# Gating one head later and dividing the next panel later, inside a projection woven with gated linear attention

## The reference

```
h = half_ffn(h, ..., w_up[0], w_down[0]);  hc likewise        # SwiGLU
n = modulate(rms_norm(h));  p = split(n @ w_in)               # q k v | gq gk gv gz | low | gate
attn = block_attention(rope(rms(q)), [rope(rms(k_lat)), rms(k_ctx)], v)
gla  = gla_chunked(forward) + flip(gla_chunked(backward))     # 4 heads, dk 64, dv 128
gla  = rms_norm(gla, g_gla) * silu(gz)
h = h + gate * ((sig(g0)*(attn @ wb0) + sig(g1)*(gla @ wb1)) @ w_out)
h = half_ffn(h, ..., w_up[1], w_down[1]);  return rms_norm(h)
```

## Time and profile before

| | us |
|---|---|
| median of 3 runs | 2684.03 (2683.47 to 2684.93) |
| profiled execution, its own time | 2686.08 |
| its span, first to last instruction | 2684.3 |
| TensorE busy | 2617.3 (98%) |
| VectorE busy | 1557.8 (58%) |
| ScalarE busy | 755.7 (28%) |
| GpSimd busy | 619.1 (23%) |
| mean granted TensorE clock | 0.992 |

### The profile page before, as it was taken

The page is one execution under the profiler, slowest core; times in us unless marked ns, Lnnn a source line. Parts: engine busy times, 40 slices in busy tenths (PEclk is TensorE's granted clock), DMA queues, the critical chain, the costliest instruction groups (busy, mean ns, idle before and its releaser), DMA issues.

```text
span 2684.3 us, 36625 instructions
## 1 busy us (share of the span) xinstructions
PE 2617.3 (98%) x14328; PEld 2170.7 (81%) x14328; DVE 1557.8 (58%) x2445; ACT 755.7 (28%) x1293; POOL 619.1 (23%) x600
## 2 busy tenths in 40 slices
PE   7999999999999999999999989999999999999998
PEld 5888888888888877877777778888778888888887
DVE  5545554444434446347674578886548666666665
ACT  3100000000000024233346568772023223222224
POOL 1064456554540000003440027560000000000001
PEclk8999999999999999999999999999999999999999
DMA  6322112222221103112224210004501111111122
GB/s 228 117 67 67 63 52 83 91 75 95 71 79 40 40 19 115 55 59 60 71 77 127 92 48 1 1 17 157 157 16 47 47 51 60 56 52 47 47 63 87
DMA packets 198293, 187.73 MB, mean 70 GB/s; under 512 B 7645, under 2 KB 149770, under 8 KB 198026
## 3 DMA queue, kind: packets, MB, share of 16 engines
q1 hardware_dynamic: 190160, 171.83, 20.2%
q10 hardware_dynamic: 7994, 13.97, 1.4%
HBM read 161.39 MB, written 24.38 MB: 69 GB/s over the span
## 4 chain that ended last, share of the span: by engine, by line
PE 89%; DVE 5%; ACT 3%; issue 1%; DMA 1%; ACTq 0%; POOL 0%; SPq 0%; DVEq 0%; POOLq 0%
PE psum L222 21%; PE psum L223 21%; PE psum L224 21%; PE psum L1089 5%; PE psum L1090 5%; PE psum L1087 5%; PE psum L2408 2%; PE psum L2428 1%; PE psum L2427 1%; PE psum L2018 1%; DVE ptl L2535 1%; ACT pth L2484 1%; PE psum L2382 1%; PE psum L2383 1%; PE psum L430 1%
## 5 line engine op out<-in xcount | busy, mean ns | idle before, releaser
L222 PE MATMUL psum<-nh,wh 128*128 128x512 f32 (+2 forms) x1688 | 629.7, 373 | 6.1 <-DVE nl L569 5.0
L223 PE MATMUL psum<-nl,wh 128*128 128x512 f32 (+2 forms) x1688 | 614.7, 364 | 0.0
L224 PE MATMUL psum<-nh,wl 128*128 128x512 f32 (+2 forms) x1688 | 614.1, 364 | 0.0
L222 PEld LDWEIGHTS psum<-nh,wh 128*128 128x128 f32 (+1 forms) x1688 | 317.9, 188 | 71.2 <-issue 10.8
L223 PEld LDWEIGHTS psum<-nl,wh 128*128 128x128 f32 (+1 forms) x1688 | 318.0, 188 | 52.8 <-issue 4.1
L224 PEld LDWEIGHTS psum<-nh,wl 128*128 128x128 f32 (+1 forms) x1688 | 317.5, 188 | 52.7
L222 PE MATMUL psum<-hidh,wh 128*128 128x512 f32 (+1 forms) x880 | 329.7, 375 | 2.6 <-DVE h L895 2.0
L223 PE MATMUL psum<-hidl,wh 128*128 128x512 f32 (+1 forms) x880 | 326.4, 371 | 0.0
L224 PE MATMUL psum<-hidh,wl 128*128 128x512 f32 (+1 forms) x880 | 325.4, 370 | 0.0
L862 ACT ACTIVATE silu_a<-psum 128x512 f32<-128x512 f32 (+1 forms) x66 | 34.7, 527 | 836.1 <-PE psum L224 836.1
L197 DVE CAST wh<-raw 128x1024 fp32r<-128x1024 f32 (+1 forms) x111 | 83.0, 748 | 322.0 <-PE psum L224 321.8
(11 more groups left out here) (345 smaller groups left out, 4757.5 us busy)
## 6 DMA issues: line engine op xcount, KB each, us to landing
raw<-in_w_ffn_up_dram SPq DMA_DIRECT2D x88, 512.0 KB, 3.9
mod_part<-in_w_mod_dram SPq DMA_DIRECT2D x96, 256.0 KB, 4.2
raw<-in_w_ffn_down_dram SPq DMA_DIRECT2D x44, 512.0 KB, 3.4
raw<-in_w_in_dram SPq DMA_DIRECT2D x34, 512.0 KB, 3.8
mod_raw<-in_w_mod_dram SPq DMA_DIRECT2D x12, 1024.0 KB, 10.6
gates_saved<-staged ACTq DMA_DIRECT2D x40, 256.0 KB, 2.0
merge_gate<-gates_saved SPq DMA_DIRECT2D x8, 1024.0 KB, 5.4
x_rows<-in_x_dram SPq DMA_DIRECT2D x8, 512.0 KB, 8.4
```

The costliest lines, as they stand in the source:

```text
L222: pe.matmul(o, hi_w, hi_x, start=first, stop=False)
L223: pe.matmul(o, hi_w, lo_x, start=False, stop=False)
L224: return pe.matmul(o, lo_w, hi_x, start=False, stop=last)
```

## The change

Two things move in VectorE's stream; no instruction is added or taken away. The second head of each group (par 1) is gated two half-units later, at `OUT_SLOTS` + 7 = 95, 104, 113, 122; the first stays where both were. And the split of the next panel, which stood ahead of all pieces of a panel's first half-unit, now stands behind them, ahead of those of the second half-unit.

```diff
@@ win_dve
         for u in range(PAIR_UNITS, N_UNITS):
             i, c = win_units[u]
-            if c == 0 and i + 1 < len(win):
-                split_panel(dve, pn(panel0 + i + 1), KT * win[i + 1][1])
             for h in (2 * u, 2 * u + 1):
                 decay_dve(dve, h)
                 state_dve(dve, h)
                 intra_dve(dve, h)
                 qk_dve(dve, h)
                 first_dve(dve, h)
+                if h == 2 * u and c == 0 and i + 1 < len(win):
+                    split_panel(dve, pn(panel0 + i + 1), KT * win[i + 1][1])
@@ intra_dve
-        if h - 5 in OUT_SLOTS:
-            g = OUT_SLOTS.index(h - 5)
-            dve.wait_ge(z_loaded, 16 + 32 * (g + 1))
-            for par in range(2):
+        for par, later in ((0, 5), (1, 7)):
+            if h - later in OUT_SLOTS:
+                g = OUT_SLOTS.index(h - later)
+                dve.wait_ge(z_loaded, 16 + 32 * (g + 1))
                 dve.wait_ge(o_rs, 2 * g + par + 1)
                 dve.wait_ge(g_oc, 2 * g + par + 1)
                 nc.vector.scalar_tensor_tensor(gla_f[:, par, :], gla_f[:, par, :], cols_b[:, B_GGLA:B_GGLA + 1],
```

## The result

| | before | after |
|---|---|---|
| median of 7 runs, us | 2684.03 (2682.11 to 2685.68) | 2691.93 (2690.31 to 2695.16) |
| span of the profiled execution | 2684.3 | 2689.0 |
| its own time | 2686.08 | 2690.77 |
| mean granted clock | 0.992 | 0.994 |

The ratio of the times is 1.0027, with a 95% interval of 1.0018 to 1.0037: slower, by 7.9 us of medians.

A forecast was written before the change was run, and what follows sets the result against it. TensorE, with 89% of the chain of waits, was taken as the bound. The terms -4.1 + 1.3 + 0.5 + 1.4 + 5.7 gave +4.8 us, set against the median 2684.03: 2688.8, range 2681.0 to 2693.5.

The forecast's parts named there:

- h=82 to 87: Panels at h=82 and 86: splits hidden before now delay h=83 and h=87; +1.3 us, from +0.2 to +1.8.
- h=94 to 97: Group 0: the 3.42 us stall and slow clock go, smaller stalls come at h=95 and 96; -4.1 us.
- h=102 to 105: Group 1: the 1.41 us stall at h=103 grows by up to 0.7; +0.5 us, from -0.4 to +1.2.
- h=110 to 115: Group 2: the split loses ScalarE's cover at h=110, making h=111 late; +1.4 us, from +0.4 to +2.0.
- h=122, 123: Group 3: late store delays the rope table, stalling h=123's permutation 4.3 us plus slow clock; +5.7, from +2.2 to +7.2.
- The rule of shared interfaces: Moved splits: GpSimd and VectorE contend for SBUF interfaces, so splits put into GpSimd's work are dear; about 0.7 us a place.
- The rule that an idle array falls to half clock: TensorE at h=123: an idle array drops to half clock, so the new stall pays twice; 2.4 us added.
- my bound for a change that can be told: Whole kernel: 0.2%, 5.4 us, is about what a measurement tells from no change.
- (a): The forecast: h=94's stall traded for one at h=123, plus small ones at splits; 2686 to 2691.5, chance 0.55.
- (b): Slower by more: splits cost 2.6 or more each, rope table late, clock falls; +9.2, 2693, chance 0.30.
- (c): Rope table in time by 1444.0, no stall at h=123; -0.9, 2683.1, or 2681.4 with all h=94 gained; chance 0.15.
- (d): The change does nothing; rejected because VectorE's order changes at nine panels; no separate chance given.

The follow-up runs named there:

- fewer_splits: The whole change, but the last group's heads both gated at h=120 and the splits of h=82, 86, 110 left ahead of their pieces: 2682.84 us, ratio 0.9991.
- before_again: The kernel before, unchanged, run once more for a second profile: 2683.36 us (one run).
- placed: Kernel before with second heads of groups 0 and 1 late and only h=94's split moved, behind the pieces of h=97: 2681.41 us, ratio 0.9988.
- placed2: As placed, with the split of h=86 also moved, behind the pieces of h=88: 2680.78 us, ratio 0.9984 against the kernel before.
- h94_only: Kernel before with only group 0's second head gated at h=95 and h=94's split behind its pieces: 2682.07 us, ratio 0.9991.
- all_again: The whole changed kernel run once more, against the kernel before: 2691.31 us, ratio 1.0026.
- rope_ahead: The whole change with the last group's heads in swapped order and the rope loads issued ahead of the last store: 2686.25 us, ratio 1.0004 against before.
- g3_only: Kernel before with only the last group's second head gated at h=122 instead of 120, splits as before: 2690.36 us, ratio 1.0020.
- gates_only: Kernel before with all four second heads gated two half-units later, every split left ahead: 2692.85 us, ratio 1.0026.
- splits_only: Kernel before with every split moved behind its panel's first pieces, both heads gated at one place as before: 2688.42 us, ratio 1.0011.

## Why the prediction was right, and where a size was off

**What bounds the kernel.** Right: TensorE still holds most of the chain of waits (the page of the changed kernel, to be read against the earlier trace rows):

```profile
PE 87%; DVE 6%; ACT 3%; issue 2%; DMA 2%; ACTq 0%; POOL 0%; SPq 0%; DVEq 0%; POOLq 0%
```

**The terms**, read as the shift of TensorE's items between the two profiled executions, place by place:

| place | predicted | after against before |
|---|---|---|
| h=82 to 87 | +1.3 | +1.8 |
| h=94 to 97 | -4.1 | -3.4 |
| h=102 to 105 | +0.5 | +0.3 |
| h=110 to 115 | +1.4 | +1.4 |
| h=122, 123 | +5.7 | +5.7 |
| sum | +4.8 | +5.8 |

The third row is read up to the output of h=106; at h=105 itself it was +0.6.

From h=81 (1253.60 and 1252.37) to h=128's permutation (1467.21 and 1471.91) it is 213.61 before and 219.54 after, +5.9. At h=81, ahead of all these places, the changed kernel's execution was already 1.2 us ahead, which gives the 4.7 of the spans. Two executions of the kernel before differ by 1.7 at the same item, so this 1.2 is no more than what separates executions, and that the spans come so near to the forecast of +4.8 is in part luck.

- **h=94 to 97.** The long wait and the clock went, 1.40 us stands at h=95, as worked out (1.4). At h=96 it is 0.86 and not 0.4, and 0.20 is left at h=94. In the window from h=95 to h=96, GpSimd (3.71 us, the fifth sum) works beside VectorE again, and the clock is 1.00 behind a wait of 1.40:

```profile
1318.95:1323.92 4.97, 4.11 (x28) 3.15 (x28) 4.94 (x7) 0.79 (x2) 3.71 (x4) 1.00 0.86 247
```

- **h=82 to 87.** 1.55 at h=83, where 1.4 was forecast; h=87's wait is 0.95, more than the 0.55 that went at h=86. A wait of 0.24 at h=82, which the prediction did not count, went too. The rule of shared interfaces (the Trainium skill, GPSIMD Engine Reference, table of the specification): the trace agrees for the subtraction, `eq` and `ek` (1.63, 1.21 and 1.10 us), and shows nothing of it for this cast (0.68).
- **h=102 to 105 and h=110 to 115.** 0.85 and 1.48 at h=102 and 103 (0.86 and 1.41 before): the wait at h=103 grew by 0.07 and not by up to 0.7, and one of 0.48 is new at h=105, as the prediction allowed. At h=111 it is 1.31: there the cover of ScalarE was lost as at h=82, and fewer_splits, which keeps that split ahead, gets it back.
- **h=122, 123.** The chain was right in each link: gate, store, rope loads, rotation, split, norm. The parts came out differently from the sum. The gating began 1.0 us earlier than I took, the loads took 0.5 longer, and the table landed at 1448.0 (1448.2 predicted). TensorE was due 0.8 earlier (1452.59 - 4.77 = 1447.82, for 1448.64), so that the wait was 4.77 and not 4.3, and the clock cost 1.4 and not 2.4. That 1.4 is 5.18 us from h=123's permutation to h=124's sums, against 4.35 before (1448.64 in the earlier trace rows to 1452.99), of which 0.56 was idle. The windows of the changed kernel show where it was: from h=123 on the clock is 0.53, and 1.00 from 1455.85.

```profile
1452.59:1455.85 3.26, 3.26 (x6) 1.97 (x7) 1.08 (x2) 1.80 (x3) 0.00 (x0) 0.53 0.67 161
1455.85:1457.77 1.92, 1.92 (x10) 1.55 (x9) 1.85 (x4) 0.00 (x0) 0.00 (x0) 1.00 0.00 0
```

Of the stall 0.56 was absorbed at h=124, where ScalarE's squares had been late before and were no longer; at h=126 nothing was. I had looked for it at h=126 and taken 1.0.

The rule that an idle array falls to half clock (the Trainium skill, TensorE: Matmul & The Clock Gate, Part 1): in this stage the traces agree at eight waits and differ at one, of 3.41 us, with the clock at 1.00 behind it. Behind these waits, from 2.2 to 5.8 us, the loss was 0 (before_again), 1.4, 1.4, 1.5, 1.6, 1.6, 2.5, 2.7 and 2.9; behind the waits of 1.3 to 1.7 us that I looked at there was none. Outside the stage they differ more often: the clock was 1.00 behind 2.24 us (the kernel before, and the changed one) and 0.61 behind 2.47 (before_again).

**The sum against the median.** The forecast was 2688.8, the median 2691.93: 3.1 us above it and 2.5 beyond my bound for a change that can be told. By place and by execution the 3.1 are: +1.1 for the places (5.9 between the two profiles against 4.8), -1.2 for what lies ahead of h=81, and 2.05 + 1.16 for the two profiled executions against their medians. The own time of the profiled execution before was 2.05 us above its median, that of the changed kernel's 1.16 below its own, and so the 4.7 us between the profiles make 4.7 + 2.05 + 1.16 = 7.9 between the medians.

The step of the prediction that was off is thus the setting of the sum against the median. It took the medians of both kernels to lie 2.05 us below their profiles, while the sum itself, in its first term of -4.1, holds the whole loss of clock of 2.4 us that one execution had behind h=94. The trace of before_again shows that the same program can do without that loss, and placed and placed2 gained by medians what is left of their sums without it. h94_only points the same way, with 2.7 us where the term says 4.1, but its interval holds both. How often an execution of the kernel before pays at h=94 is open.

The 1.16 on the other side is not in that term. The mean granted clock of every execution of the changed kernel is on record, 15 in all with all_again: the six at 0.994 or 0.995 took 2690.0 to 2691.2 us, the two at 0.993 2691.4 and 2691.9, the five at 0.992 2691.5 to 2693.1, and the two at 0.991 2695.2 and 2695.4. Both profiles of the changed kernel are of executions at 0.994 and 0.995. So slower executions are those with a lower clock, and the profiles show two that lost little to it; 1.4 us behind h=123, where 2.4 had been forecast, is probably less than what the median pays, but no profile of a slower one was taken, and where they lose it is not shown.

**The rivals.** The mechanism is (a)'s. The median lies 0.4 us above the upper end of (a)'s own range (2691.5), and is nearer to (b)'s 2693 than to the forecast, for another reason than (b) gave: the splits did not cost 2.6 everywhere. That the change is slower by more than the 5.4 us taken as noise had been given 0.45. (c) needed the table by 1444.0; it landed at 1448.0, and rope_ahead, where it is in time, measured what (c) says in kind: level with before. (d) is out.

## What to carry to other kernels

Before an instruction is moved later, follow its semaphore into the queues of the other engines: here a store of one head, which nobody was waiting for, held back a table load in SyncE's in-order queue, and that made a change that is otherwise level 0.27% slower (rope_ahead, with the loads ahead of the store, is level again). Work that an engine does while it waits for another engine's result anyway is free only at that place; behind the result it delays what follows (1.55 us at h=83). A better place for it is where the critical engine does something long that does not ask for this engine: in placed2 the wait at h=95 is gone, and the kernel, with two of the heads late as well, is 0.16% faster than before. A gain that rests on a low clock in one profiled execution should be priced from several executions, since the same wait was followed once by 2.5 us of loss and once by none.

## What the runs showed of the hardware that was not expected

The granted clock behind the same wait is not the same in every execution: 3.42 us of idle were followed by 0.58 until the next item, 3.41 us in another execution of the same program by 1.00. In g3_only the same 3.42 us cost 1.6. A longer wait did not cost more either: 4.77, 4.80 and 5.82 us cost 1.4, 1.6 and 1.4, and 3.16 us cost 2.9. A shorter one can cost too: a wait of 1.91 us for ScalarE's `ktok`, between 1189 and 1196 us (L1884 in the kernel before), is in every profile here, and in the 7 us behind it the clock was 0.76 in gates_only, splits_only and h94_only and 1.00 in the kernel before (both executions), the changed one (both) and g3_only. What decides it is open; no run here was made for it.
